# Turning the SSD output later in the next chunk of a two-block Trainium2 kernel

## What is computed

```python
decay_ls = exp(where(causal, a_cs[l] - a_cs[s], -inf))
y_diag   = einsum('lsg,lsge,sgep->lgep', C @ B.T, decay_ls, X)
states   = einsum('lgn,lge,lgep->gepn', B, exp(a_cs[-1] - a_cs), X)
h_next   = h * exp(a_cs[-1]) + states            # carried from chunk to chunk
y_off    = einsum('lgn,gepn,lge->lgep', C, h, exp(a_cs))
y = (y_diag + y_off + d_skip * xs) * silu(z)
y = rmsnorm(y, norm_w)
```

## Time and profile before

| | |
|---|---|
| Time, median of 3 runs | 1842.21 us (1839.58 to 1843.87) |
| Time of the profiled execution | 1842.98 us |
| Its span | 1841.1 us |
| PE busy | 1746.5 us, 95% of the span |
| DVE busy | 695.8 us, 38% |
| ACT busy | 326.7 us, 18% |
| Mean granted TensorE clock | 0.970 |

### The profile page before, as it was taken

How to read it: one execution, slowest core, us unless ns; L and a number is a source line. 1 busy time by engine, 2 the same in 40 slices (tenths; PEclk the granted TensorE clock), 3 DMA queues, 4 the chain that set the end, 5 groups by cost and what they waited for, 6 DMA issues and landing times.

```text
span 1841.1 us, 18442 instructions
## 1 busy us (share of the span) xinstructions
PE 1746.5 (95%) x7264; PEld 962.0 (52%) x7264; DVE 695.8 (38%) x1575; ACT 326.7 (18%) x679; POOL 18.7 (1%) x39
## 2 busy tenths in 40 slices
PE   6999899979999999989999988999979999999997
PEld 3445444468888854435544544444454544545452
DVE  4322348666777711030698223212241211112123
ACT  1121224221111100010233423210210000000000
POOL 0001000000000000000000000000000000000001
PEclk8999999989999999999899989999989999999999
DMA  9675110011222122132111110132369999999997
GB/s 401 244 299 192 46 59 33 32 46 46 91 91 91 69 112 94 63 125 91 52 46 46 46 46 1 46 132 97 126 279 405 430 429 428 430 429 428 429 428 310
DMA packets 30239, 335.50 MB, mean 182 GB/s; under 512 B 3208, under 2 KB 5784, under 8 KB 10592
## 3 DMA queue, kind: packets, MB, share of 16 engines
q1 hardware_dynamic: 22464, 310.56, 41.8%
q10 hardware_dynamic: 5168, 14.91, 2.1%
q0 software_dynamic: 2544, 9.18, 1.4%
HBM read 319.66 MB, written 18.37 MB: 184 GB/s over the span
## 4 chain that ended last, share of the span: by engine, by line
PE 81%; DMA 7%; DVE 7%; ACT 3%; issue 1%; SPq 0%; POOL 0%; DVEq 0%; ACTq 0%; POOLq 0%
PE bank L960 14%; PE bank L1312 14%; PE bank L605 10%; PE bank L996 8%; PE bank L1121 6%; PE bank L1321 5%; PE bank L1129 3%; PE bank L777 3%; PE bank L1079 2%; DMA arena<-in_w_expert_up 2%; DMA upper<-in_w_expert_up 2%; DMA slot<-in_w_expert_up 2%; PE bank L919 2%; PE bank L587 2%; PE bank L767 2%; PE bank L937 2%
## 5 line engine op out<-in xcount | busy, mean ns | idle before, releaser
L1312 PE MATMUL bank<-slot,arena 128*64 128x512 f32 x704 | 234.5, 599 | 4.7 <-DMA upper<-in_w_expert_up 2.2
L1312 PE MATMUL bank<-upper,arena 128*64 128x512 f32 x352 | 157.8, 604 | 2.7 <-DMA arena<-in_w_expert_up 2.7
L996 PE MATMUL bank<-arena,slot 128*128 128x512 f32 x352 | 151.2, 592 | 0.0
L605 PE MATMUL bank<-hT,slot 128*128 128x512 f32 x272 | 125.8, 622 | 8.0 <-DVE hT L1841 6.5
L1121 PE MATMUL bank<-hT,slot 128*128 128x512 f32 x256 | 120.9, 621 | 11.8 <-ACT arena L2200 10.4
L1321 PE MATMUL bank<-arena 128*128 128x128 f32 x1024 | 123.8, 280 | 8.5 <-DVE arena L2094 8.5
L1321 PEld LDWEIGHTS bank<-arena 128*128 128x128 f32 x1024 | 119.5, 196 | 20.8 <-issue 12.2
L1312 PEld LDWEIGHTS bank<-slot,arena 128*64 128x64 f32 x704 | 73.0, 138 | 105.8 <-issue 99.9
L2127 DVE TENSOR_TENSOR arena<-arena,bank 128x512 f32<-128x512 f32 x16 | 11.0, 689 | 281.9 <-PE bank L1312 281.9
L996 PEld LDWEIGHTS bank<-arena,slot 128*128 128x128 f32 x352 | 66.9, 190 | 83.8 <-issue 83.7
L605 PEld LDWEIGHTS bank<-hT,slot 128*128 128x128 f32 x272 | 53.4, 200 | 78.2 <-issue 74.0
(11 more groups left out here) (400 smaller groups left out, 2224.9 us busy)
## 6 DMA issues: line engine op xcount, KB each, us to landing
slot<-in_w_expert_gate SPq DMA_DIRECT2D x17, 2048.0 KB, 24.6
slot<-in_w_expert_down SPq DMA_DIRECT2D x16, 2048.0 KB, 28.0
slot<-in_w_in SPq DMA_DIRECT2D x15, 2048.0 KB, 8.1
slot<-in_w_ada SPq DMA_DIRECT2D x12, 2048.0 KB, 13.4
slot<-in_w_up SPq DMA_DIRECT2D x11, 2048.0 KB, 8.1
slot<-in_w_expert_up SPq DMA_DIRECT2D x11, 2048.0 KB, 23.4
upper<-in_w_expert_up SPq DMA_DIRECT2D x11, 2048.0 KB, 27.0
upper<-in_w_expert_down SPq DMA_DIRECT2D x6, 2048.0 KB, 28.6
```

The costliest lines, as they stand in the source:

```text
L605: ins = pe.matmul(bank[home[g]][:, :], w[:, k, c0:c0 + P], src[:, k, :], start=(k == 0), stop=(k == KD - 1))
L996: ins = pe.matmul(bank[j][:, :], w[:, k, :], actT[:, k, :], start=(k == 0), stop=(k == FT - 1))
L1312: ins = pe.matmul(dst[b * CAP:(b + 1) * CAP, :], lhs(b, k), rhs(b, k), start=(k == 0), stop=(k == n_k - 1))
```

## The change

On TensorE, `turn_y(c - 1)` moves from the head of chunk c to behind `decays(c + 1)`, `states(c)` and two of the products of the projections. Two products fewer are issued behind `outputs` in chunks 1 and 2, and four more behind `outputs` of the last chunk; the total stays 96. On VectorE, `exponents(c + 1)` comes ahead of `y_turned(c - 1)`.

```diff
                 for c in range(1, NT):
-                    turn_y(c - 1)
                     fill(4)
                     if c + 1 < NT:
                         decays(c + 1)
                     states(c)
-                    fill(6)
+                    fill(2)
+                    turn_y(c - 1)
+                    fill(4)
                     outputs(c)
-                    fill(8 if c + 1 < NT else 10)
+                    fill(6 if c + 1 < NT else 14)
                 turn_y(NT - 1)
...
                     if c + 1 < NT:
                         inputs(c + 1)
+                    if c + 1 < NT:
+                        exponents(c + 1)
                     if c >= 1:
                         y_turned(c - 1)
-                    if c + 1 < NT:
-                        exponents(c + 1)
```

## The result

| | before | after |
|---|---|---|
| Median of 8 runs | 1841.74 us (1834.76 to 1843.87) | 1826.78 us (1825.19 to 1833.19) |
| Ratio of the runs, 95% interval | 1 | 0.9944 [0.9925, 0.9963] |
| Span of the profiled execution | 1841.1 us | 1829.4 us |
| Its mean granted clock | 0.970 | 0.973 |

The kernel is 0.56% faster by the ratio, some 10 us. Why medians and ratio differ by 5 us is told under the experiments: the times of both kernels fall into two groups.

What follows compares the result with a forecast made beforehand. TensorE's own stream was taken to bound the kernel. Waits of 5.89 us plus 1.69 of clock, 7.58, took 1842.98 to 1835.4, or 1834.6 for the median; forecast 1835.0, range 1831.0 to 1838.5 (its own 1832.5 to 1837.5).

Steps and rivals of the forecast that it cites:

- The cause of the waits: SSD scan: y is late because ScalarE's root stands behind emptying banks; TensorE's turn waited 8.3 us in four waits.
- The replay: Scan's new order on TensorE: turns at 203.9, 224.0, 242.0; y has 4.8, 4.8 and 2.8 us spare.
- The waits' term: TensorE's first three turns in the scan: waits of 3.53, 1.82 and 0.54 removed, 5.89 us.
- The clock term in the scan: First turn and fill(4): the half-clock stretch behind the first wait goes, 1.69 us, by the page in some runs only.
- the sum: Scan: waits of 5.89 us and clock of 1.69 us, together 7.58 us.
- What was at nothing: VectorE's swap only keeps cover, and four more products behind the last chunk buy nothing by themselves.
- ScalarE's emptying: Scan: Q0 and K3 find their banks emptied in time, so no wait.
- The last wait: Last turn: stays at 2.44 us, since root(3) stands behind Q3's emptying.
- A: Behind the last wait: the half-clock stretch vanishes too, 7.6 plus up to 2.9 us gained, 1832; chance 14%.
- B: Last stage: gain given back to loads started by something that does not move; 1839 half absorbed, 1842 wholly; chance 11%.
- C: Third turn: y(2) over 2.8 us later than replayed, so a wait stays; 1837 at 2 us; chance 3%.
- D: Scan: late y delays outputs and the next y, chunk to chunk; slower, 1846; chance 3%.

Runs made afterwards that it cites:

- the version with the root first: Changed kernel with ScalarE's root of the last chunk ahead of emptying Q3 and the last turn ahead of the last two products: 0.9914 to before.
- an added delay of 6.5 us: Changed kernel with nine idle VectorE passes, 6.5 us in all, ahead of the normalised y of chunks 0 to 2: 1.0000 to before.
- the kernel that works through its waits: Kernel before with 4, 2, 0 and 3 unused TensorE products ahead of the four turns: 0.9950 to before.
- the faster profile of before: Second further profile of the unchanged kernel before, which fell into the faster group: 1835.75 us, clock 0.977.
- the repeat: The changed kernel run again, unaltered, as the measure for the experiments: 0.9937 to before.
- the two kernels with unused products: Kernel before with unused products ahead of its turns, 0.9950; changed kernel with 3 ahead of its last turn only, 0.9937; both to before.

## Why the prediction was right, point by point

**The cause of the waits.** Right for the two long ones, and in part for the others. At chunk 0 ScalarE squares y(0) only behind K0's emptying, and K0's last product is the last ahead of the turn; at the last chunk it is Q3, and the version with the root first shows it (the wait gone). That the change removed three waits shows that y came late, not why. The rows of ScalarE before say more on the middle two:

```profile
...
220.97 0.60 ACT L2200 ACTIVATE upper<-bank 128x512 f32<-128x512 f32 x1 [8.92 <-PE bank L777]
221.46 0.62 ACT L2200 ACTIVATE arena<-arena 128x512 f32<-128x512 f32 x1
...
242.86 0.60 ACT L2200 ACTIVATE upper<-bank 128x512 f32<-128x512 f32 x1 [8.56 <-PE bank L777]
243.79 0.63 ACT L2200 ACTIVATE arena<-arena 128x512 f32<-128x512 f32 x1 [0.33 <-DVE arena L1674]
```

y(1) was gated at 220.14 and squared at 221.46, behind K2: the queue cost some 1.3 of the 1.82 us, an estimate from these rows. y(2) was squared as soon as VectorE had gated it (L1674); ScalarE had already emptied Q0 and stood 0.33 us. The wait of 0.54 us came from VectorE's work behind the outputs, not from the queue. In the new order the emptying is the later of the two each time (K2 emptied from 216.15, y(1) squared at 216.64; Q0 from 236.01, y(2) at 236.50), as the replay had it, so its times don't suffer from this.

**The replay.** It had the four turns at 203.9, 224.0, 242.0 and 263.0; with the start 0.6 us later, they came at 204.28, 224.14, 241.82 and 262.96. y had 4.55, 4.55 and 2.37 us of spare where 4.8, 4.8 and 2.8 stood. The units were some hundredths of a microsecond too long; an added delay of 6.5 us met that spare, with waits of 1.88, 1.88 and 4.05.

**The waits' term.** 5.89 us, all gone, as read.

**The clock term in the scan.** 1.69 forecast, 1.67 in the kernel that works through its waits. In the faster profile of before, too, the fill of four behind the first turn took 5.29 us, at half clock for the most part, where it takes 3.60 at full. Each of the four profiles with the wait of 3.53 us had a half-clock stretch behind it, so there the 1.69 us were due in both groups, not in some runs only. Elsewhere equal waits were followed by different stretches: 109 and 113 us at half clock in all against 83. The rule cited in the prediction from the Trainium skill (TensorE: Matmul & The Clock Gate, "What's actually happening") is that the switch depends on where the work falls in a free-running cycle. These sums agree with it, but not with the prediction's use of it on the 1.69 us.

**The step that was mis-sized: the sum.** 7.58 us were forecast for the scan and 8.23 measured. The missing 0.65 is what a wait costs beside its idle time. Where a turn doesn't wait it starts 0.16 us ahead of the modelled end of the product before it (204.28 against 202.56 + 1.88), and the product behind follows 0.43 us on instead of 0.50: three times 0.16 + 0.07 is 0.69. I had only counted the idle time.

**What was at nothing.** VectorE's swap and the four products behind the last chunk: right, each shown by a kernel of its own. ScalarE's emptying: right, no product of the projections (L777) waits for it in the timeline after.

**The last wait.** Right that it stays, and why: from Q3's emptying to the turn it is 2.40 us before (268.18 to 270.58) and after (260.56 to 262.96).

**The rivals.** A (the clock behind the last wait) did not come by itself: the repeat's profile still has that stretch whole, and the first profile of the kernel after has half of it. From the last turn to the attention's first products of 512 columns (L668) it is 11.30 us before, 10.33 after and 11.53 in the repeat. In the two kernels with unused products it is 8.69, 2.8 less than in the repeat: the bound of 2.9 was right for this stretch. Behind the last turn as a whole both have 5.3 us less (1556.8 and 1556.6, against 1562.1 and 1561.9), since stretches further on, at about 364 and 402 us, were shorter or missing as well. B: nothing was given back, 0.2 us behind the scan at a like clock, and the waits for the experts' weights are 12.1 us in the repeat for 12.4 in the faster profile of before. But the wait of 79.0 us that the prediction set against B lies within the scan (SP waiting for the products of L777), not from 270 us on. Over the whole span SP's waits for TensorE's later lines are larger still (395.3 us in 44 waits for L1312), so what it was to show holds. C and D: no wait was left, and the added delay showed no chain.

**The time.** 1835.0 was set against a median of 1842.2. I took the spread of the three runs, 4.3 us, for noise on a median of some 2 us. It is not: the kernel has two levels 7.7 us apart, and the three runs shown, like the profile, came from the slower one. That is why the median lies below the range though the scan's gain is nearly as forecast. It was luck, too, that the ratio's 1831.4 fell on the inner side of 1831.0: its interval reaches 3.5 us to either side, and it is nearer to A's 1832 than to 1835.0, though A's mechanism did not do it.

## What to carry to other kernels

When an engine waits at the head of a step, replay the streams and look for the instruction that the late one is queued behind. Here it was mostly a copy out of a bank on ScalarE, and four products issued first would have covered it. How far the consumer then moves may depend on what else lies in the row: once, light matmuls side by side were followed by the half clock as a wait is. Compare timings within a level of the granted clock, or by many runs: a few runs of two kernels may differ by 7 us for nothing. And a wait of TensorE that can't be removed can be worked through with products that nobody uses; here that was worth some 6 us at a like clock, and no wait was shorter.

## What the runs showed of the hardware

- The same program has times in two groups, 7.7 us apart, with mean granted clocks of 0.969 to 0.974 and 0.977 to 0.979, at the same waits in the scan to 0.01 us. In the profiles the time at half clock was 109 and 113 us against 83.
- TensorE fell to half clock without a wait: busy 3.31 of 3.40 us with transposes, 8-row and 256-column matmuls, then 0.51 for 3.4 us. The same row of matmuls 23 us later kept 1.00.
- A wait of 2.44 us was followed by the half clock in some profiles at once and in others some microseconds later: after, the turn behind it took 0.66 us at full clock and the matmuls at 265 us ran at 0.57 (windows below); one of 1.82 us never was.

```profile
...
265.00:269.00 4.00, 3.89 (x9) 0.57 0.99 422
```

- Nine unused products in the waits were worth 0.50% of the kernel's time [0.25, 0.74] by the ratio, and 6.2 us within the faster group. In the profiles 1.7 us lie in the scan and 2.6 to 2.8 right behind the last wait; why stretches further on were shorter or missing stays open.
